# The first stage of a two-layer decoder kernel: both key groups of the memory as one group, 512 columns wide

## What is computed

```python
for i in range(2):
    h = rms_norm(x, pre_norm[i])
    proj = h @ w_in[i]                     # token columns | 512 memory-query columns | 2048 gate columns
    tok_out = short_conv(...) if i == 0 else diff_attention(...)
    mem_n = rms_norm(mem, mem_norm[i])
    km, vm = split(mem_n @ w_kv_mem[i])    # 512 key columns, 512 value columns, 4 heads of 128
    cross_out = softmax(q_mem @ km.T * 128 ** -0.5) @ vm
    y = concat(tok_out, cross_out) * silu(gate) @ w_out[i]
    x = x + rms_norm(y, post_norm[i])

def rms_norm(x, g):
    return x * rsqrt(mean(x * x) + 1e-6) * g
```

## Time and profile before

| | us |
|---|---|
| median of 3 runs | 961.33 (960.43 to 962.17) |
| the profiled execution | 961.81 |
| its span, first to last instruction | 959.8 |
| TensorE busy | 942.2 |
| VectorE busy | 629.6 |
| ScalarE busy | 476.5 |

### The profile page before, as it was taken

The page is one execution under the profiler, slowest core; times in us unless marked ns, Lnnn a source line. Parts: engine busy times, 40 slices in busy tenths (PEclk is TensorE's granted clock), DMA queues, the critical chain, the costliest instruction groups (busy, mean ns, idle before and its releaser), DMA issues.

```text
span 959.8 us, 14019 instructions
## 1 busy us (share of the span) xinstructions
PE 942.2 (98%) x5129; PEld 809.8 (84%) x5129; DVE 629.6 (66%) x872; ACT 476.5 (50%) x720; POOL 1.2 (0%) x9
## 2 busy tenths in 40 slices
PE   6999999999999999999999999999999999999996
PEld 5888888888888888888888888888888888888885
DVE  4777656666665666655596447457878878886555
ACT  6866544444434444344465445435465465554441
POOL 0000000000000000000000000000000000000000
PEclk9999999999999999999999999999999999999999
DMA  9666465566666565666566656565655765746562
GB/s 313 218 220 216 143 209 175 175 199 189 203 193 187 188 195 185 207 196 195 183 217 194 192 154 195 159 204 168 197 178 156 221 180 164 206 147 204 191 194 90
DMA packets 149690, 182.30 MB, mean 190 GB/s; under 512 B 8017, under 2 KB 118929, under 8 KB 148881
## 3 DMA queue, kind: packets, MB, share of 16 engines
q1 hardware_dynamic: 148704, 177.25, 59.6%
q10 hardware_dynamic: 944, 4.49, 1.3%
HBM read 176.48 MB, written 2.10 MB: 186 GB/s over the span
## 4 chain that ended last, share of the span: by engine, by line
PE 96%; DVE 1%; ACT 1%; issue 1%; DMA 1%; DVEq 0%; ACTq 0%
PE psum L345 42%; PE psum L346 21%; PE psum L374 9%; PE psum L373 9%; PE psum L372 9%; PE psum L391 1%; PE psum L542 1%; PE psum L416 1%; PE psum L399 1%; DMA cross_gate<-in_mem_norm_dram 1%; PE psum L514 0%; PE psum L408 0%; DVE memT_split L849 0%; PE psum L525 0%; PE psum L524 0%
## 5 line engine op out<-in xcount | busy, mean ns | idle before, releaser
L345 PE MATMUL psum<-hT_split,hi_ring 128*128 128x512 f32 x1600 | 560.0, 396 | 0.0
L821 DVE TENSOR_TENSOR lo_ring<-raw_ring,hi_ring 128x1024 fp32r<-128x1024 f32 x320 | 387.2, 1223 | 251.5 <-ACT hi_ring L591 248.4
L591 ACT ACTIVATE hi_ring<-raw_ring 128x1024 fp32r<-128x1024 f32 x320 | 337.6, 1062 | 401.0 <-PE psum L346 266.2
L346 PE MATMUL psum<-hT_split,lo_ring 128*128 128x256 f32 x1600 | 444.6, 278 | 0.0
L345 PEld LDWEIGHTS psum<-hT_split,hi_ring 128*128 128x128 f32 x1600 | 300.1, 188 | 70.8 <-issue 2.0
L346 PEld LDWEIGHTS psum<-hT_split,lo_ring 128*128 128x128 f32 x1600 | 300.9, 188 | 0.1
L372 PE MATMUL psum<-hi_ring,branchT_split 128*128 128x512 f32 x256 | 99.9, 390 | 0.0
L374 PE MATMUL psum<-hi_ring,branchT_split 128*128 128x512 f32 x256 | 99.6, 389 | 0.0
L373 PE MATMUL psum<-lo_ring,branchT_split 128*128 128x512 f32 x256 | 99.6, 389 | 0.0
L373 PEld LDWEIGHTS psum<-lo_ring,branchT_split 128*128 128x128 f32 x256 | 48.1, 188 | 10.0
L374 PEld LDWEIGHTS psum<-hi_ring,branchT_split 128*128 128x128 f32 x256 | 48.0, 188 | 10.0
(11 more groups left out here) (169 smaller groups left out, 623.7 us busy)
## 6 DMA issues: line engine op xcount, KB each, us to landing
raw_ring<-in_w_in_dram SPq DMA_DIRECT2D x224, 512.0 KB, 4.2
raw_ring<-in_w_out_dram SPq DMA_DIRECT2D x64, 512.0 KB, 4.9
raw_ring<-in_w_kv_mem_dram SPq DMA_DIRECT2D x32, 512.0 KB, 5.5
layer_area<-layer_area SPq DMA_DIRECT2D x48, 64.0 KB, 3.2
stage_area<-in_mem_dram SPq DMA_DIRECT2D x4, 512.0 KB, 7.7
x_residual<-in_x_dram SPq DMA_DIRECT2D x1, 2048.0 KB, 10.7
x_residual<-in_x_dram ACTq DMA_DIRECT2D x1, 2048.0 KB, 8.4
layer_area<-in_post_norm_dram ACTq DMA_DIRECT2D x2, 1024.0 KB, 5.4
```

Source lines behind the costliest of these rows:

```text
L345: mm(o, hi[:, k, P * c:P * (c + 1)], X[:, kt, :], start=kt == 0, stop=False)
L346: last = mm(o[:, SEQ:], lo[:, k, P * c:P * (c + 1)], X[:, kt, 0:SEQ], start=False, stop=kt == KT - 1)
L591: run(whi[:, slot, :], raw[:, slot, :], ACT.Copy).then_inc(hi_ready, 1)
L821: V_.tensor_tensor(wlo[:, slot, :], raw[:, slot, :], whi[:, slot, :].bitcast(f32), SUB)\
```

## The change

The two key groups become one, `first_keys`, over all 512 key columns in banks 0 to 3, with k outermost: unit n now holds k tiles 2n and 2n + 1 at 512 columns, so that it needs the turn of memory step n alone. The number of key matmuls stays 64 pairs.

- SyncE loads the memory in eight pieces of 256 columns, one with each unit; the first unit in two halves; x in two halves behind units 6 and 7.
- ScalarE issues the mem-norm rows first, then the pre-norm rows; TensorE turns them apart, the mem-norm rows at the start (waiting only for them), the pre-norm rows inside the value group, ahead of its third unit (`rows_turn`), together with the two small products.
- TensorE makes ten transposes of the identity whose result nobody reads ahead of the gain turn, and eight more behind the turn of step 0 (`idle_turns`). It turns step n + 1 ahead of unit n's matmuls. The last unit is worked by tiles, (0, 1) and then (2, 3), with a semaphore of its own after the first.
- The plain copies of memory steps are shared: even steps ScalarE, odd steps VectorE.
- ScalarE's order behind the key stage is: squares, high part, squares, high part, squares of x, high part, small terms of tiles 0 and 1, squares of x, high part, small terms of tiles 2 and 3.
- VectorE has one rsqrt chain for the memory's two and x's two columns (`token_stats`), behind the first sum of keys. `scale_x` and `take_row` change places.

The diff, cut to its core:

```diff
+        def first_keys(w):
+            w = w.rearrange("(k p) n -> p k n", p=P)[:, :, 0:CROSS_WIDTH]
+            load_mem(0)
+            sp.dma_start(raw[:, 0, 0:CROSS_WIDTH], w[:, 0, :]).then_inc(unit_begun, 16)
+            sp.dma_start(raw[:, 0, CROSS_WIDTH:], w[:, 1, :]).then_inc(raw_loaded[0], 16)
+            for n in range(1, STEPS):
+                load_mem(n)
+                unit(n, n % SLOTS, raw[:, n % SLOTS, :].rearrange("p (k c) -> p k c", k=K_KT),
+                     w[:, K_KT * n:K_KT * (n + 1), :])
+                if n >= STEPS - TT:
+                    load_x(n - (STEPS - TT))
...
+            pe.wait_ge(tr_lo, N_MEM0 + 1)
+            pe.wait_ge(lo_begun, 1)
+            k_tile(0, 0, range(4))
+            mem_turn(1)
+            pe.wait_ge(lo_ready, 1)
+            k_tile(0, 1, range(4)).then_inc(unit_done, 1)
+            for n in range(1, STEPS - 1):
+                mem_turn(n + 1)
+                pe.wait_ge(tr_lo, N_MEM0 + n + 1)
+                pe.wait_ge(lo_ready, n + 1)
+                for k in range(K_KT):
+                    last = k_tile(n, k, range(4))
+                last.then_inc(unit_done, 1)
...
+            for tiles, done in (((0, 1), keys_half), ((2, 3), unit_done)):
+                for k in range(K_KT):
+                    last = k_tile(STEPS - 1, k, tiles)
+                last.then_inc(done, 1)
...
-        mem_turns(0, 1, 2, 3)
-        column_group(G_KM0, U_KM0, 0, XB, x_steps=N_MEM0,
-                     at={1: lambda: mem_turns(4, 5), 2: lambda: mem_turns(6, 7)})
-        column_group(G_KM0 + 1, U_KM0 + B_UNITS, 1, XB)
+        mem_turn(0)
+        idle_turns(8)
+        first_keys(XB)
...
-        act.dma_start(norm_rows[0:32, :], pre_norm.rearrange("l (k p) -> (l k) p", p=P)).then_inc(rows_loaded, 16)
-        act.dma_start(norm_rows[32:64, :], mem_norm.rearrange("l (k p) -> (l k) p", p=P)).then_inc(rows_loaded, 16)
+        act.dma_start(mem_rows, mem_norm.rearrange("l (k p) -> (l k) p", p=P)).then_inc(mem_rows_loaded, 16)
+        act.dma_start(pre_rows, pre_norm.rearrange("l (k p) -> (l k) p", p=P)).then_inc(pre_rows_loaded, 16)
...
+        def take_keys(i):
+            act.wait_ge(*((unit_done, STEPS) if i else (keys_half, 1)))
+            if i:
+                act.wait_ge(bank_free, 1)
+            run(small, banks(i)[:, :, SEQ:], ACT.Copy).then_inc(small_copied, 1)
...
+        def combine_keys(i, lows):
+            dve.wait_ge(lo_ready, lows)
+            dve.wait_ge(small_copied, i + 1)
+            V_.tensor_tensor(kmT[:, 2 * i:2 * i + 2, :], banks(i)[:, :, 0:SEQ], small, ADD).then_inc(bank_free, 1)
+        low(STEPS, 3)
+        combine_keys(0, STEPS + 3)
+        token_stats()
+        low(STEPS, 4, 3)
+        combine_keys(1, STEPS + 4)
```

More of the change, by code:

```diff
@@ L23 @@
 B_KT = KT // B_UNITS
+K_KT = UNIT // CROSS_WIDTH
 A_KT = KT // A_UNITS
@@ L348, in column_group, with first_keys, k_tile @@
                 last.then_inc(unit_done, 1)
+        def first_keys(X):
+            def k_tile(n, k, tiles):
+                kt = K_KT * n + k
+                at = slice(CROSS_WIDTH * k, CROSS_WIDTH * (k + 1))
+                hi, lo = whi[:, n % SLOTS, at], wlo[:, n % SLOTS, at]
+                for c in tiles:
+                    mm(ps[:, c, :], hi[:, P * c:P * (c + 1)], X[:, kt, :], start=kt == 0, stop=False)
+                    last = mm(ps[:, c, SEQ:], lo[:, P * c:P * (c + 1)], X[:, kt, 0:SEQ], start=False, stop=kt == KT - 1)
+                return last
+            pe.wait_ge(tr_lo, N_MEM0 + 1)
[11 more added lines that the diff above has]
+                last.then_inc(unit_done, 1)
+            pe.wait_ge(tr_lo, N_MEM0 + STEPS)
+            pe.wait_ge(lo_ready, STEPS)
+            for tiles, done in (((0, 1), keys_half), ((2, 3), unit_done)):
+                for k in range(K_KT):
+                    last = k_tile(STEPS - 1, k, tiles)
+                last.then_inc(done, 1)
         def row_group(G, u, s, X, order, before=None, at={}, half_first=False):
@@ L424, in _, with idle_turns, mem_turn @@
         pe.wait_ge(const_ready, 3)
[L425 to L434, removed]
+        def idle_turns(n):
+            for _ in range(n):
+                nc.tensor.transpose(ps[:, 6, 0:P], ident, ident)
+        idle_turns(10)
+        pe.wait_ge(mem_rows_loaded, 16)
+        nc.tensor.transpose(ps[:, 7, 0:32], mem_rows, ident[0:32, 0:32]).then_inc(norm_turned, 1)
+        def mem_turn(n):
+            pe.wait_ge(mem_loaded[n], 16)
+            if n == 3:
+                pe.wait_ge(norm_ready, 1)
+            turn(N_MEM0 + n, mem_raw)
         def turns_of(first, steps, src, ready=None):
@@ L442, in turns_of, with rows_turn @@
             return run
-        mem_turns(0, 1, 2, 3)
-        column_group(G_KM0, U_KM0, 0, XB, x_steps=N_MEM0,
-                     at={1: lambda: mem_turns(4, 5), 2: lambda: mem_turns(6, 7)})
-        column_group(G_KM0 + 1, U_KM0 + B_UNITS, 1, XB)
[L449 to L453, removed]
+        mem_turn(0)
+        idle_turns(8)
+        first_keys(XB)
+        def rows_turn():
+            pe.wait_ge(diag_ready, 2)
+            pe.wait_ge(tr_lo, STEPS)
+            pe.wait_ge(pre_rows_loaded, 16)
+            nc.tensor.transpose(ps[:, 7, 256:288], pre_rows, ident[0:32, 0:32]).then_inc(norm_turned, 1)
+            for t in range(TT):
+                last = mm(ps[:, 7, P * t:P * (t + 1)], ones, diag[:, P * t:P * (t + 1)], start=True, stop=True)
+            last.then_inc(row_done, 1)
         def x_ready():
@@ L904, in op, with first_low, keep, token_stats @@
             st.need()
-        for n in range(STEPS):
+        def first_low(half):
+            dve.wait_ge(*((hi_ready, 1) if half else (hi_begun, 1)))
+            part = slice(CROSS_WIDTH * half, CROSS_WIDTH * (half + 1))
+            V_.tensor_tensor(wlo[:, 0, part], raw[:, 0, part], whi[:, 0, part].bitcast(f32), SUB)\
+              .then_inc(lo_ready if half else lo_begun, 1)
+        def keep(n):
+            dve.wait_ge(tr_lo, n + 1)
+            V_.tensor_copy(memT[:, 2 * n:2 * n + 2, :], ps[:, 4 + n % 4, :].rearrange("p (k t) -> p k t", k=2))\
+              .then_inc(kept_odd, 1)
+        turned(N_MEM0, XB, 2 * KT)
+        first_low(0)
+        first_low(1)
+        for n in range(1, STEPS):
+            low(0, n + 1, n)
             turned(N_MEM0 + n, XB, 2 * KT)
             if n % 2:
-                low(0, n // 2 + 1, n // 2)
-        column_group(G_KM0, 0, U_KM0, 0, kmT[:, 0:2, :])
-        def mem_stat():
+                keep(n)
+        def token_stats():
             dve.wait_ge(mem_squared, 2)
-            rsqrt(st, mem_rstd, ss[:, 0:2], D_MODEL)
+            dve.wait_ge(x_squared, 2)
+            rsqrt(st, both_rstd, ss[:, 0:4], D_MODEL)
             st.need()
```

101 lines of the change are left out of this document (63 added, 38 removed).

## The result

The changed kernel is **slower: 966.03 us** (median; 965.46 to 966.41) against 961.26 (960.43 to 962.17) measured beside it, a ratio of 1.0045 with a 95% interval of 1.0033 to 1.0057. The forecast was 965.2 with a range of 962.6 to 967.4.

A forecast was written before the change was run, and what follows sets the result against it. TensorE, busy 98% of the span, bounds the kernel. End of keys -2.7, wait for x -1.1, small passes 0, bank wait +6.3, clock +1.35: query group 3.85 us later, forecast 965.2 us, range 962.6 to 967.4.

The forecast's parts named there:

- First matmul: Start of the key stage: TensorE's first key matmul at 8.6 us instead of 11.78, not held up by idle turns.
- Key stage: The 64 key pairs: 22.3 us of matmuls, 3.0 of turns and 0.3 of waiting, at the high clock.
- the loop of two steps: Key stage: ScalarE and VectorE pass work in 6.5 us against TensorE's 6.4, costing 0.1 to 0.6, taken as 0.3.
- So I take the low level and E = 35.4: E, end of the keys: 35.4 us with TensorE first at 1.2 GHz for 2.7 us; 34.2 at high clock.
- rival (1): Start of key stage: idle turns bring the clock up, keys end 1.2 us earlier, time 964.0; chance 0.20.
- Bank wait: Between keys and value group: TensorE waits 6.3 us for banks 0 and 1, behind squares in ScalarE's queue.
- the lower bound of 5.9: Wait for banks after the keys: 5.9 us if ScalarE has taken the last turns 4.6 us before the keys' end.
- Clock in the wait: Start of value group: clock falls during the wait and stays low for 2.7 us, losing 1.35 us.
- The upper bound of 2.5: Clock loss at the value group's start: at most 2.5 us, if low nearly twice as long.
- No wait for x: Value group, turns of x: TensorE no longer waits for VectorE's scaled x, saving 1.1 us.
- Rival (4): Between keys and value group: bank wait is short, 0.2 us, and the clock holds, time 957.7; chance 0.06.
- Behind 68.79 all shifts along: From the query group on: the program is unchanged and all shifts by its start, forecast 3.85 us later.

The follow-up runs named there:

- e5: The changed kernel as it is, measured a second time: 965.7 us, ratio 1.0042 to the kernel before.
- e2: The changed kernel without its 18 idle turns: 966.64 us, ratio 1.0046.
- e6: The e4 kernel (squares rearranged) without its 18 idle turns: 959.07 us, ratio 0.9973.
- e4: The changed kernel, memory's squares moved partly into the key stage, small terms copied after one high part, later value-group work rearranged to match: 957.86 us, ratio 0.996.
- e3: The changed kernel with 44 more idle turns between the last key matmul and the value group's first: 963.27 us, ratio 1.0018.
- e1: The changed kernel with the small terms of key tiles 0 and 1 copied behind one square and one high part, not three each: 963.24 us, ratio 1.0012.
- e8: The changed kernel with the two norm-gain DMAs in the old order, pre-norm first: a single run, 969.55 us.
- e7: The changed kernel with the first square of x put behind the copy of small terms instead of ahead: 964.16 us, ratio 1.0022.

## Why the prediction was right, point by point

The sign, the size and the main mechanism were right, but the sum was closer than its terms. That only 0.8 us lie between the forecast of 965.2 and the 966.03 is in part luck. In its own trace the query group came 3.4 us later where the forecast said 3.85: the keys ended 1.03 earlier than forecast (34.37 for 35.4), the wait was 0.32 shorter (5.98 for 6.3), and the clock cost 0.90 more (2.25 for 1.35), which makes 3.85 - 1.03 - 0.32 + 0.90 = 3.4. The rest is the spread of medians, 4.8 us apart in the first comparison and 3.8 in e5's. Errors of both signs cancelled.

- **First matmul, 8.6 forecast, 8.28 measured.** Right in size and partly by luck: the step took 3.6 us for the first row DMA, and it was 2.3 here. But the idle turns, which the step said don't hold this up, held TensorE until 4.24, a microsecond beyond the rows. e2 and e6 show that: the gain turn starts at 3.78 and 3.23 without them. The first pair lost less by it (8.09 and 7.80), because memory piece, ScalarE and VectorE are late as well.
- **Key stage, 25.6 at the high clock forecast, 26.1 measured.** Close; the loop of two steps held TensorE once, for 0.4 us at 12.4.
- **"So I take the low level and E = 35.4": this step failed.** Its argument was the sixteen transposes ahead of slow matmuls in before. In after TensorE was at the high level from the first pair, as rival (1) had it, and E was 34.37. What the idle turns are worth in the median is open: 1.2 us by e4 and e6, which is what rival (1) gave for them, but next to nothing by e2 beside after. The Trainium skill (TensorE: Matmul & The Clock Gate, Part 4: PE-mode transpose) says that transposes don't bring the full clock. Here the measurement decides against it: in e3 only 44 transposes stood in the gap, and the clock stayed at 1.00 where it fell to 0.51 without them. And in e4 the eight idle turns at 5.32 took 1.04 us, against 1.92 in after, so the high level had come when TensorE had made nothing but transposes. What the sixteen turns of before lacked is not settled; they stood between 6.58 and 10.55, with 1.2 us of idle time behind them. In e1 and e8 the 23 turns now ahead of the first pair were not enough either.
- **Bank wait, 6.3 forecast, 5.98 measured.** Right, near the lower bound of 5.9, for the reason that the bound gave: ScalarE was through with the last turns at 29.7, 4.7 before E, not 4.2. From there to the value group it took 10.66 us, forecast 10.5. The working for the rest held: 8.5 us for three squares and three high parts (29.69 to 38.21), forecast 8.6. e7 shows the queue as the cause, e4 takes the wait away.
- **Clock in the wait, 1.35 forecast, 2.25 measured: the term that was mis-sized.** That it falls was right, from 5.3 us at the kernel's end; here it took 3.7. The loss was taken from the 2.7 us at the start, but the way back took 4.5 us of matmuls. The upper bound of 2.5 held in after; with the 5.3 us of e7 and the 5.6 of e8 it would not have. e3 measures the loss by itself as 2.1.
- **No wait for x: right.** The diagonals came at 43.2 to 43.7, and TensorE asked at 48.1, later than forecast because of the slow clock. e1 shows what lay behind: once TensorE was early, the chain behind the squares became the next wait, 3.4 us. Rival (4), a short bank wait, priced at 957.7 what it would bring; e4 measured 957.86, with some luck, since there the keys ended 0.9 before the 35.4 and the value group followed 0.6 behind them, not 0.2. Rival (4) asked for less time in the whole queue, which would have brought the diagonals forward too. e1 shows that moving the copy alone is not enough.
- **Behind 68.79 all shifts along**: right, up to 0.4 us.

## What to carry to other kernels

When groups that took turns in a scarce resource (here banks 0, 1 and 2, 3) are fused into one that holds all of it, look for what frees it and count everything that stands ahead of that in the in-order queues; the other group was its cover. Price the wait, then ask what is late next once it is gone (e1), and move independent work to where its engine has room (e4) rather than behind it. Here a gap of 5.98 us in TensorE's work cost more than its length: 2.1 to 2.25 us on top, by the clock.

## What the hardware showed that I had not expected

- **Transposes alone held the clock, and brought it.** 44 transposes of the identity in the gap kept it at 1.00 (e3). The eight at 5.39 took 1.92 us in after and 1.04 at 5.32 in e4, so in e4 the clock was up before the first product.
- **The clock fell sooner and came back later than the places in before suggested, and neither is one figure.** After the last matmul it fell at 2.8 us (e7), 3.3 (e5), 3.5 (e1), 3.7 (after), 4.1 (e2) and 4.7 (e8), where the kernel's end in before had 5.3. It came back behind 3.3 us of matmuls (e1), 4.2 (e5), 4.5 (after), 4.9 (e2), 5.3 (e7) and 5.6 (e8), where the start of before had 2.7.
- **The same program starts at either level.** Five of seven traces with idle turns had the high clock at the first key pair; the profile's clock column says 1.00 at the start in either case, and only the spacing tells.
- **The same small DMA lands at very different times.** The first of the gain rows took 3.6 us in before, whose memory pieces are 512 KB, and 2.3 to 3.1 in the nine traces with pieces of 256 KB; the second 4.9, and 2.9 to 4.6. Whether the size of the pieces makes the difference is not shown: before has one trace, and no run changed the pieces alone.
